# Latent attention heads: the rotated score products of the second token half on other row groups of TensorE

## The reference, cut to what matters

```
def apply_rope(x, cos, sin):
    half = x.shape[-1] // 2
    x1, x2 = x[..., :half], x[..., half:]
    return jnp.concatenate([x1 * c - x2 * s, x2 * c + x1 * s], -1)

# dense_attention: ql is the rotated query, qc the same query without rotation
s = jnp.concatenate([jnp.einsum('bqhd,bkhd->bhqk', qc, k_ctx),
                     jnp.einsum('bqhd,bkhd->bhqk', ql, k_lat)], -1)
p = softmax_f32(s.astype(jnp.float32) * scale)
```

## Time and profile before

| | us |
|---|---|
| median of 3 runs | 1832.21 (1832.12 to 1832.63) |
| the profiled execution | 1831.41 |
| its span in the profile | 1829.6 |
| PE busy | 1674.6 (92%) |
| DVE busy | 1028.7 (56%) |
| ACT busy | 392.6 (21%) |
| share of PE in the chain that ended last | 78% |
| share of DMA in the chain that ended last | 18% |

### The profile page before, as it was taken

One profiled execution on the slowest core, in us unless ns is written; L12 is line 12 of the kernel. 1 busy time (PEld: TensorE's weight loads), 2 busy tenths in 40 slices (PEclk: granted clock), 3 DMA queues, 4 the chain that ended last, 5 costly groups with the idle time before them and its releaser, 6 DMA issues.

```text
span 1829.6 us, 34612 instructions
## 1 busy us (share of the span) xinstructions
PE 1674.6 (92%) x14868; PEld 1337.2 (73%) x14868; DVE 1028.7 (56%) x2171; ACT 392.6 (21%) x1001; POOL 0.2 (0%) x4
## 2 busy tenths in 40 slices
PE   7999999999999999999999999999998766757666
PEld 4565687888888886776899998788887555545554
DVE  1499979888867327887699874565423111111111
ACT  0344323221210114222222203113402100000001
POOL 0000000000000000000000000000000000000000
PEclk9999999999999999999999999999999888888988
DMA  9423324322231214654344533333479999999996
GB/s 391 182 81 116 135 113 156 138 113 114 91 141 32 118 47 158 246 171 189 139 154 169 227 120 139 139 139 116 169 320 369 426 428 428 428 429 429 428 427 290
DMA packets 36464, 395.44 MB, mean 216 GB/s; under 512 B 3968, under 2 KB 7296, under 8 KB 15232
## 3 DMA queue, kind: packets, MB, share of 16 engines
q1 hardware_dynamic: 36352, 393.84, 53.5%
HBM read 392.77 MB, written 1.05 MB: 215 GB/s over the span
## 4 chain that ended last, share of the span: by engine, by line
PE 78%; DMA 18%; DVE 2%; issue 1%; ACT 0%; SPq 0%; DVEq 0%
PE bank L2145 14%; PE bank L1855 13%; PE bank L715 13%; DMA ring<-w_moe 10%; DMA arena<-w_moe 7%; PE bank L1583 7%; PE bank L4083 3%; PE bank L2422 3%; PE bank L2468 3%; PE bank L1013 2%; PE bank L3849 2%; PE bank L2418 1%; PE bank L1318 1%; PE bank L769 1%; PE bank L4094 1%; PE bank L3075 1%
## 5 line engine op out<-in xcount | busy, mean ns | idle before, releaser
L1855 PE MATMUL bank<-arena,ring 128*128 128x256 f32 (+1 forms) x940 | 167.4, 336 | 0.0
L1855 PEld LDWEIGHTS bank<-arena,ring 128*128 128x128 f32 x940 | 148.0, 191 | 14.5 <-issue 0.4
L4235 DVE TENSOR_TENSOR arena<-arena,bank 128x128 f32<-128x128 f32 x32 | 9.2, 288 | 223.7 <-PE bank L4083 223.7
L4083 PE MATMUL bank<-arena 128*32 128x128 f32 x2008 | 78.2, 319 | 53.4 <-DMA arena<-w_moe 50.5
L2145 PE MATMUL bank<-arena 128*128 128x256 f32 x504 | 115.7, 379 | 0.0
L4083 PEld LDWEIGHTS bank<-arena 128*32 128x32 f32 x2008 | 67.4, 129 | 65.1 <-DMA arena<-w_moe 60.5
L715 PE MATMUL bank<-layer_input,ring 128*128 128x256 f32 x496 | 111.5, 381 | 0.0
L2145 PEld LDWEIGHTS bank<-arena 128*128 128x128 f32 x504 | 95.7, 190 | 13.2 <-DVE arena L2286 0.2
L715 PEld LDWEIGHTS bank<-layer_input,ring 128*128 128x128 f32 x496 | 92.8, 190 | 15.0 <-issue 2.8
L4083 PE MATMUL bank<-ring,arena 128*32 128x128 f32 x1920 | 67.9, 302 | 32.6 <-DMA ring<-w_moe 32.6
L4083 PEld LDWEIGHTS bank<-ring,arena 128*32 128x32 f32 x1920 | 58.4, 122 | 43.1 <-DMA ring<-w_moe 37.1
(11 more groups left out here) (571 smaller groups left out, 3099.1 us busy)
## 6 DMA issues: line engine op xcount, KB each, us to landing
arena<-w_moe SPq DMA_DIRECT2D x45, 2048.0 KB, 25.8
ring<-w_moe SPq DMA_DIRECT2D x45, 2048.0 KB, 26.5
ring<-w_ffn_in SPq DMA_DIRECT2D x13, 2048.0 KB, 8.1
ring<-w_ffn_in SPq DMA_DIRECT2D x7, 3072.0 KB, 10.0
ring<-w_proj SPq DMA_DIRECT2D x7, 3072.0 KB, 10.4
ring<-w_ffn_out SPq DMA_DIRECT2D x6, 2816.0 KB, 9.9
ring<-w_na_pair SPq DMA_DIRECT2D x5, 2048.0 KB, 8.2
arena<-w_far SPq DMA_DIRECT2D x16, 512.0 KB, 5.5
```

What stands on the lines that cost most here:

```text
L1855: last = eng.matmul(out, w[:, k * P:(k + 1) * P], x[:, k, :], start=(start and k == 0), stop=(stop and k == half - 1), skip_group_check=True)
L4083: ins = eng.matmul(bank[x][group[q], 0:P], xe[:, k, SLOTS * e:SLOTS * e + SLOTS], weight(e, first, last, (x * KT + k) * FE + q * P, P), st ...
```

## The change

Half t = 1 of the rotated products goes from row groups `far` to `own`, where half t = 0 stays on `far`. In the plain products of L1293 the halves trade places. The rotated query of the second half thus needs no swap: a third constant, `own_mla`, is the rotation without the move; cosine is applied to `un` itself for this half. The swap constant works on the first half alone, and `swapped` holds that half. The table of masks loses a part that was zero, and the table of constants shrinks from 4364 to 3660 columns of 128 partitions.

```
-          ("nsa_mask", 416), ("cmp_keep", 32), ("level_mask", (len(LEVELS) + 1) * P), ...
+          ("nsa_mask", 416), ("cmp_keep", 32), ("level_mask", (len(LEVELS) + 1 - WHOLE) * 32), ...
         def rotate(g):
-            pe.matmul(b[:, 0:LAT], self.con("swap_mla"), v["un"][:, CTX:T], start=True, stop=True)
-            pe.matmul(b[:, LAT:2 * LAT], self.con("rot_mla"), v["un"][:, CTX:T], start=True, stop=True)\
+            pe.matmul(b[:, 0:P], self.con("swap_mla"), v["un"][:, CTX:CTX + P], start=True, stop=True)
+            pe.matmul(b[:, LAT:LAT + P], self.con("rot_mla"), v["un"][:, CTX:CTX + P], start=True, stop=True)
+            pe.matmul(b[:, LAT + P:2 * LAT], self.con("own_mla"), v["un"][:, CTX + P:T], start=True, stop=True)\
                 .then_inc(s["rot_done"], 1)
             def rotated(t):
                 for j in range(2):
-                    ins = pe.matmul(bank[2 + 2 * t + j][:, CTX:T], sw[far[j], t * P:(t + 1) * P], kp[far[j], CTX:T],
+                    r = (far[j], own[j])[t]
+                    ins = pe.matmul(bank[2 + 2 * t + j][:, CTX:T], sw[r, t * P:(t + 1) * P], kp[r, CTX:T],
                                     start=True, stop=False, skip_group_check=True)
             def plain(t):
                 for j in range(2):
-                    x, r = (v["swapped"][far[j], :], far[j]) if t else (un[own[j], CTX:CTX + P], own[j])
+                    x, r = (un[own[j], CTX + P:T], own[j]) if t else (v["swapped"][far[j], :], far[j])
         def rotated(g):                                   # on VectorE
-            dve.tensor_tensor(v["sw"], b[:, 0:LAT], self.con("cos_mla"), ALU.mult)
-            dve.tensor_copy(v["swapped"], b[:, P:LAT])
+            dve.tensor_tensor(v["sw"][:, 0:P], b[:, 0:P], self.con("cos_mla", 0, P), ALU.mult)
+            dve.tensor_tensor(v["sw"][:, P:LAT], v["un"][:, CTX + P:T], self.con("cos_mla", P, P), ALU.mult)
+            dve.tensor_copy(v["swapped"], b[:, 0:P])
             dve.tensor_tensor(v["roped"], b[:, LAT:2 * LAT], self.con("sin_mla"), ALU.mult).then_inc(taken, 1)
+    c["own_mla"] = rotation(groups, DR // 2, P)
```

More of the change, by code:

```diff
@@ L69 @@
 WHOLE = 2
-CONSTS = [("ident", P), ("ones", P), ("slot", SLOTS), ("before", P), ("ahead", P), ("first4", GROUPS), ("mean", P), ("rot_mla", P), ("swap_mla", P), ("cos_mla", LAT), ("sin_mla", LAT),
+CONSTS = [("ident", P), ("ones", P), ("slot", SLOTS), ("before", P), ("ahead", P), ("first4", GROUPS), ("mean", P), ("rot_mla", P), ("swap_mla", P), ("own_mla", P), ("cos_mla", LAT), ("sin_mla", LAT),
           ("rot_nsa", P), ("cos_nsa", LAT), ("sin_nsa", LAT),
-          ("nsa_mask", 416), ("cmp_keep", 32), ("level_mask", (len(LEVELS) + 1) * P), ("scan_keep", LAT),
+          ("nsa_mask", 416), ("cmp_keep", 32), ("level_mask", (len(LEVELS) + 1 - WHOLE) * 32), ("scan_keep", LAT),
           ("cmp_fold", 16), ("spread", 4 * P), ("fold24", 24)]
@@ L4479, in constants @@
     own = [np.tile(m[0:32, 0:32], (4, 1)) for m in masks[WHOLE:]]
-    c["level_mask"] = np.concatenate(own + [np.zeros((P, (len(LEVELS) + 1) * P - 32 * len(own)))], 1)
+    c["level_mask"] = np.concatenate(own, 1)
     c["scan_keep"] = np.broadcast_to((tok % 64 != 0), (P, LAT))
```

## The result

The changed kernel takes 1835.05 us in the median of 12 runs (1834.02 to 1839.03), the kernel before 1832.16 in 12 runs beside them (1830.18 to 1832.89). The ratio is 1.002, with a 95% interval of 1.0012 to 1.0029, so it is 2.2 to 5.3 us slower; the medians are 2.9 apart. The forecast was 1834.4, in a range of 1831.5 to 1836.2.

What follows compares the result with a forecast made beforehand. PE's own stream was taken to bound the heads' stage, except turn 7, set by DVE's chain. 2.58 + 0.35 - 0.57 - 0.15 = +2.21 us on the median of 1832.21 gave 1834.4 us, range 1831.5 to 1836.2.

Steps and rivals of the forecast that it cites:

- Exchange of row groups: Heads' stage, turns 1 to 6: two more rounds on `own` cost 0.43 us a turn, 2.58 us in all.
- L1288 starts twice: Sign in turns 1 to 7: two records beside L1282's first, then more four rounds later on `own`.
- Turn 7: Last turn of heads: L1293 ends 0.43 us later, 0.08 is slack, DVE's chain carries the other 0.35 us.
- Rotation products: Six 128-column records replace four of 256, 0.67 us for 0.86: 0.19 less a quad, 0.57 us over turns 1, 3, 5.
- Turn 0: First turn of heads: gains about 0.15 us, as the late L1286 had left `own` idle there.
- VectorE: Chain to `roped`: two 128-column multiplications for one of 256 add 0.07 us, covered by slack; at most 0.6 us if dear.
- Carrying it to the end one for one: From the heads' stage to the end: every shift of the heads arrives in full; about 2.2 us expected at 1380 us.
- Constants: Opening: a table 0.36 MB smaller changes the time by 0, being queued behind the first weights PE waits for.
- the forecast's own range: Whole kernel: +1.9 to +3.0 us and half a microsecond between runs, so 1833.3 to 1835.7 us.
- A: 32-row products, heads' stage: starts keep program order over all row groups, so -0.6 us, 1831.6 us; chance 0.07.
- B: 32-row products, heads' stage: nothing overlapped before, so two rounds replace four, 4.0 us faster, 1828.2; chance 0.04.
- C: Last expert's work: the 1.2 GHz level reaches over L4109, adding 1.5 to 3.6 us, taken as 1836.9; chance 0.07.

Runs made afterwards that it cites:

- e4_merged: The kernel before, with L1293's plain products moved ahead of L1303, so all products of 32 rows form one block; 1833.05 us against 1832.21, ratio 1.0005.
- e9_width: The kernel before with the short mask table and 128 unused columns, so the constants have 3660 columns; 1832.90 us against 1831.84, ratio 1.0003.
- e6_same: The kernel before once more, with only a blank line added; 1832.87 us against 1832.21 for the kernel before beside it, ratio 1.0005.
- e2_far: The changed kernel with both halves' rotated products on `far` again, its three rotation products kept; 1832.49 us against 1832.60 for the kernel before, ratio 1.0000.
- e3_own: The kernel before with only the second half's rotated products moved to `own`; 1834.85 us against 1832.60, ratio 1.0011.
- e7_both: The changed kernel with all products of 32 rows merged into one block as in e4_merged; 1833.90 us against 1832.21 for the kernel before, ratio 1.0009.
- e0_after: The changed kernel run again with no edit; 1834.96 us against 1832.60 for the kernel before, ratio 1.0016.
- e8_first: e4_merged with half 0's rotated products put ahead of L1281 in program order; 1830.52 us against 1832.41 for the kernel before, ratio 0.9993.
- e1_table: The kernel before with only the mask table shortened, 832 columns less; 1833.28 us against 1832.60, ratio 1.0007.

## Why the prediction was right, and where not

**Exchange of row groups:** right in mechanism and nearly in size. Forecast 0.43 us a turn, measured 0.40 (3.65 to 4.05 from the first record to the projection). I had added two rounds to 1.09, but that contained 0.03 by which `far` started later than `own` and so decided L1303's start; now `own` decides, and L1305 follows 0.31 after its last round. Six turns gave 2.40, not 2.58. "L1288 starts twice" is there, and L1305 did not use the idle row groups.

**Turn 7:** forecast 0.35 through the chain of maxima. From L1277 to L1318 it was 205.64 to 214.13 in the chain, 8.49 us, and is now 208.94 to 217.79, 8.85: 0.36.

**Rotation products:** 0.19 a quad, as measured. **Turn 0:** forecast 0.15 gained; from L1239 to the next projection 6.07 us became 5.95: 0.12. Of this 0.09 lies between L1282 and L1305, as the forecast has it (0.08), and 0.03 ahead of L1282, where it has 0.07. **VectorE:** 0.07 forecast and measured, and covered. The sum of the parts, 2.40 + 0.36 - 0.57 - 0.12 = 2.07, meets the stage's 2.10.

**Carrying it to the end one for one:** right as far as can be seen. In the two profiles the distance from the stage to the last weights differs by 0.67 us. But over the eleven profiles whose chain passes there it is 1578.3 to 1579.3 (1580.2 in e4_merged, with its fall of the clock), with stages from 132.65 to 138.40, so the distance doesn't go by the stage.

**Constants:** this step failed, though the total doesn't show it. "0" stood on the table being queued behind the weights that PE waits for. It is queued there, but with the changed width those weights land some 0.6 us later (e9_width). The forecast of 2.2 with the 0.4 to 0.6 that arrives is 2.6 to 2.8, and the two pairs of medians say 2.9 and 2.4 (the two ratios 3.7 and 2.9). Medians of equal programs lie 0.7 apart (e6_same), so the 0.65 us by which 1835.05 lies above 1834.4 neither needs this term nor excludes it.

**Range and resolution:** the lower end of the forecast's own range, 1833.3, doesn't follow from its terms: 2.16 us with the most that turn 0 may gain, less half a microsecond, gives 1833.9. And the prediction held 3.7 us to be the least that a measurement can tell from no change; 12 runs beside 12 told a smaller one, with an interval of 2.2 to 5.3.

**Rivals:** A falls by e2_far, e3_own and e7_both; B falls, the exchange alone costs 2.7. C did not happen: in all eleven profiles whose chain passes there the last expert's products of L4112 (L4108 to L4110 in others) took 3.65 us, and the slow L4083 of the earlier trace rows was before's own, worth 1.6 us in that profile. In e0_after, e2_far and e3_own an earlier expert's 64 records took 3.42 to 3.58 us, and the wait for weights behind it was 25.6 to 25.8 us instead of 27.1; such a stretch is made up for as long as a wait follows, and behind the last one none does. I read a disturbed stretch there as the usual one; it touched only the profile's sum.

## What to carry to other kernels

In these runs products of 32 rows took turns only with those on the same row groups: count for each group the rounds between two changes of tile height, and the fullest group is the time. Four rounds took 1.09 us to the next product of 64 rows, six 1.49 to 1.51, eight 1.92. A move that fills idle groups in one list can unbalance the block that the hardware forms with its neighbour, so look in the timeline for what already runs beside it. And where a product on one group waits for one on another, put the awaited one early in the program, since here it reported no earlier than what stood ahead of it (a stall of 0.29 us a turn in e4_merged, none in e8_first).

## What the runs showed that I had not expected

Starts and reports of products differ in order: L1286's records started 0.03 us after L1281's first and ahead of six of its records, while the wait in e4_merged was met as if only when L1281, ahead of it in the program, had ended; the reordering in e8_first took the stall away. The Trainium skill ("TensorE: Matmul & The Clock Gate", section "The mechanism") has both starts and ends in program order. The starts in these traces are not, and neither are the ends as the profile gives them (L1286's first pair ends at 123.06, L1281's last at 123.68); only the reports, as far as e4_merged and e8_first show them, keep that order.

The width of the table of constants, whose DMA is queued after them, moved the landing of the first weights: 8.8 to 8.9 us or 9.4 to 9.6 by its width.

TensorE's granted clock fell to 0.50 (1.2 GHz) for some 3.4 us in turn 7 in four of thirteen profiles, the four that ran together, after a wait of 1.8 us that the others have too (1.7 to 2.0); the stage is 1.50 us longer by it in e0_after and 1.55 in e1_table. And the first 20 records of L1013 took 8.78 us in the profile of before, 9.68 in that of the change and 8.78 again in e0_after, the same program: a microsecond that no edit here explains, and one reason why single runs tell so little.
